# A fourth seven-product group per quarter in the MLP of a Trainium2 encoder block

## The reference

```python
h2 = rms_norm(x, norm_ffn_g[l])
u = jnp.square(jax.nn.relu(jnp.einsum('bsd,df->bsf', h2, w_up[l])))
x = x + jnp.einsum('bsf,fd->bsd', u, w_down[l])
return rms_norm(x, norm_final_g)
```

## Time and profile before

| | us |
|---|---|
| median of 3 runs (1476.1 to 1477.17) | 1476.41 |
| the profiled execution | 1476.14 |
| its span, first to last instruction | 1474.3 |
| PE busy, 6950 matmuls | 1464.3 |
| DVE busy | 1148.8 |
| ACT busy | 777.3 |

### The profile page before, as it was taken

One profiled execution on the slowest core, in us unless ns is written; L12 is line 12 of the kernel. 1 busy time (PEld: TensorE's weight loads), 2 busy tenths in 40 slices (PEclk: granted clock), 3 DMA queues, 4 the chain that ended last, 5 costly groups with the idle time before them and its releaser, 6 DMA issues.

```text
span 1474.3 us, 18847 instructions
## 1 busy us (share of the span) xinstructions
PE 1464.3 (99%) x6950; PEld 1275.4 (87%) x6950; DVE 1148.8 (78%) x1429; ACT 777.3 (53%) x998; POOL 15.0 (1%) x21
## 2 busy tenths in 40 slices
PE   9999999999999999999999999999999999999997
PEld 8888888888888888888888888888888888888886
DVE  7977887776577787777799766897787787889677
ACT  7656564444455555444445555555555555456553
POOL 0000000000000000000000000000000000000000
PEclk9999999999999999999999999999999999999999
DMA  9556544666655565565765777767867876777853
GB/s 327 195 169 208 185 154 166 229 202 239 212 183 183 190 199 175 193 203 199 245 233 182 251 248 239 234 210 240 268 204 218 265 244 226 243 221 234 283 192 127
DMA packets 163097, 317.69 MB, mean 215 GB/s; under 512 B 6752, under 2 KB 16608, under 8 KB 162784
## 3 DMA queue, kind: packets, MB, share of 16 engines
q1 hardware_dynamic: 149216, 297.51, 60.9%
q10 hardware_dynamic: 13824, 19.41, 4.6%
HBM read 306.41 MB, written 10.49 MB: 215 GB/s over the span
## 4 chain that ended last, share of the span: by engine, by line
PE 94%; DVE 3%; issue 1%; DMA 0%; ACT 0%; SPq 0%; DVEq 0%; POOLq 0%; POOL 0%; ACTq 0%
PE acc L619 83%; PE banks L856 5%; PE acc L909 3%; DVE wlo L1388 1%; PE acc L856 1%; PE banks L638 1%; PE banks L657 1%; PE banks L647 0%; DVE sum_lo L1984 0%; DMA raw<-in_w_in 0%; DVE mix L1988 0%; ACT whi L947 0%; DVE mix L1774 0%; DVE ta_lo L1994 0%; PE banks L754 0%
## 5 line engine op out<-in xcount | busy, mean ns | idle before, releaser
L947 ACT ACTIVATE whi<-raw 128x1024 fp32r<-128x1024 f32 x542 | 568.1, 1056 | 573.6 <-PE acc L619 480.9
L1388 DVE TENSOR_TENSOR wlo<-raw,whi 128x1024 fp32r<-128x1024 f32 x542 | 655.4, 1221 | 264.6 <-ACT whi L947 260.9
L619 PE MATMUL acc<-whi,ta_hi 128*128 128x512 f32 x1308 | 497.4, 380 | 0.3 <-DVE wlo L1477 0.3
L619 PE MATMUL acc<-wlo,ta_hi 128*128 128x512 f32 x1308 | 495.7, 379 | 0.0
L619 PE MATMUL acc<-whi,ta_lo 128*128 128x512 f32 x1308 | 495.7, 379 | 0.0
L619 PEld LDWEIGHTS acc<-whi,ta_hi 128*128 128x128 f32 x1308 | 247.2, 189 | 37.0 <-issue 1.8
L619 PEld LDWEIGHTS acc<-whi,ta_lo 128*128 128x128 f32 x1308 | 247.2, 189 | 35.0
L619 PEld LDWEIGHTS acc<-wlo,ta_hi 128*128 128x128 f32 x1308 | 247.3, 189 | 34.6
L619 PE MATMUL acc<-whi,tb_hi 128*128 128x512 f32 x512 | 194.2, 379 | 0.0
L619 PE MATMUL acc<-wlo,tb_hi 128*128 128x512 f32 x512 | 194.0, 379 | 0.0
L619 PE MATMUL acc<-whi,tb_lo 128*128 128x512 f32 x512 | 194.0, 379 | 0.0
(11 more groups left out here) (213 smaller groups left out, 1190.4 us busy)
## 6 DMA issues: line engine op xcount, KB each, us to landing
raw<-in_w_in SPq DMA_DIRECT2D x64, 1024.0 KB, 5.2
raw<-in_w_up SPq DMA_DIRECT2D x64, 1024.0 KB, 5.3
raw<-in_w_down SPq DMA_DIRECT2D x54, 1024.0 KB, 5.2
raw<-in_w_gate SPq DMA_DIRECT2D x32, 1024.0 KB, 5.4
raw<-in_w_att SPq DMA_DIRECT2D x16, 1024.0 KB, 5.0
raw<-in_w_ret SPq DMA_DIRECT2D x16, 1024.0 KB, 5.0
raw<-in_w_out SPq DMA_DIRECT2D x16, 1024.0 KB, 5.2
raw<-in_w_down SPq DMA_DIRECT2D x20, 512.0 KB, 4.7
```

What stands on the lines that cost most here:

```text
L619: last = nc.tensor.matmul(paired(acc[B.parity][:, t, :]), a[:, k, tok], halves_in_turn(b), start=(k == 0 and n == 0), stop=(k == (B.ends + ...
L947: nc.scalar.activation(whi[:, B.ring_at(u), :], raw[:, B.raw_at(u), :], ACT.Copy).then_inc(hi_ready, 1)
L1388: V_.tensor_tensor(wlo[:, at, :], raw[:, B.raw_at(u), :], whi[:, at, :].bitcast(f32), ALU.subtract).then_inc(lo_ready, 1)
```

## The change

`LATE` gets a third entry: up block 3 hosts columns 2 and 3 of c = 2. So J and K lose two more units each in quarters 0 to 2 (all four down blocks have 4 units), and the up block 3 of quarters 1 to 3 gets a group. Where J is short (4 units), DVE does the mixtures after J's first split, and J's second split behind them. In both fold functions the third fold goes ahead of the split of unit u+3, and in `fold_to_bank` two splits of K, not one, come ahead of folds 4 and 5. The loops over quarters 1 and 2 are written out.

```diff
-LATE = {0:(0,1,3),2:(0,1,2)}
+LATE = {0: (0, 1, 3), 2: (0, 1, 2), 3: (2, 3, 2)}
...
             stage6(0, True)
-            with pe.Fori(1, 3) as q:
+            for q in range(1, 3):
                 stage6(q, False)
             stage6(3, False, True)
...
                 split(Q.down[1], 3, 4)
+                short = Q.units[2] == 4
                 if not wide:
-                    split(Q.J, 0, 2)
+                    split(Q.J, 0, 1 if short else 2)
                 mixed_tokens(Q.turn(q, 4), q * MIXES_OF_QUARTER)
+                if short:
+                    split(Q.J, 1, 2)
                 lo_from_exchanged(q * 4 + 16, 3)
...
                 fold(1, G.k, acc[K.parity][:, 0, :], ALU.add)
-                split(E, u + 3, u + 4)
                 dve.wait_ge(product_done, G.products(2))
                 fold(0, G.k, chain, ALU.subtract)
-                part(K, 0, 1)
+                split(E, u + 3, u + 4)
+                part(K, 0, 2)
                 dve.wait_ge(product_done, G.products(3))
                 dve.wait_ge(folded, G.folds(2))
                 fold(1, G.k, chain, ALU.subtract)
                 fold(1, G.j, chain, ALU.add)
-                part(K, 1, 2)
+                part(K, 2, 3)
                 dve.wait_ge(folded, G.folds(5))
                 add_residual(E, G.j)
-                part(K, 2, K.ends + 1)
+                part(K, 3, K.ends + 1)
...
                 fold(1, G.k, third, ALU.add)
-                split(E, u + 3, u + 4)
                 dve.wait_ge(product_done, G.products(2))
                 fold(0, G.k, chain, ALU.subtract)
+                split(E, u + 3, u + 4)
                 dve.wait_ge(folded, G.folds(3))
                 fold(0, G.j, second, ALU.add)
                 split(B, 6, 7)
```

More of the change, by code:

```diff
@@ L585, in _ @@
             stage6(0, True)
-            with sp.Fori(1, 3) as q:
+            for q in range(1, 3):
                 stage6(q, False)
@@ L1360, in _ @@
             stage6(0, True)
-            with act.Fori(1, 3) as q:
+            for q in range(1, 3):
                 stage6(q, False)
@@ L1997, in _ @@
             stage6(0, True)
-            with dve.Fori(1, 3) as q:
+            for q in range(1, 3):
                 stage6(q, False)
```

## The result

The change is slower: 1484.33 us (1483.49 to 1485.24) against 1476.1 us (1476.06 to 1477.17), five runs each, a ratio of 1.0055 with a 95% interval of 1.0044 to 1.0066. The forecast was 1478.9, its range 1474.9 to 1481.7. The profiled execution took 1483.92 us, and its span is 7.8 us longer than that of before.

A forecast was written before the change was run, and what follows sets the result against it. PE was taken as the bound: matmuls times pitch, plus holes. Terms -3.9 - 1.3 + 2.5 + 1.8 + 1.7 + 1.95 - 0.1 = +2.65 us on 1476.14 gave 1478.8, stated as 1478.9, range 1474.9 to 1481.7.

The forecast's parts named there:

- The matmuls: New group on PE: 42 matmuls do what 48 did, three times, so 18 fewer, -3.9 us.
- the sixth product's holes: Six old late groups: with fold 3 ahead of the split, PE's wait before product six goes, -1.3 us.
- the tails: Units behind six late groups: split 7 is done too late for PE, 0.42 us each, +2.5 us.
- the last quarter: Quarter three keeps eight-unit down blocks; its sixth product is in time and its end gains, -0.1 us.
- The addition of DVE's line in the boundary group: Quarters one and two: DVE's instructions without a pause make PE wait 1.15 us each, against 0.3 before; +1.7 us together.
- quarter zero's boundary: Boundary group of quarter zero: the fetch lands later, so PE waits 2.4 us against 0.45 before, +1.95 us.
- the new late group: Fourth up block's group: the corner lands 5.2 us after issue, fold 2 is late, 0.6 us three times, +1.8 us.
- the paragraph on the boundary group: Boundary groups behind four J units: fetched tokens land by 1073.7, mixtures follow J's first split; +1.7 and +1.95 us.
- Transfers too late: Rival: late fetches and right corners delay DVE and PE pays one for one; 1484, with half 1481.5; chance 0.14.
- Rivals one and two: Whole kernel: half the waits, 1475.4 to 1477.4, chance 0.18; the waits don't appear, 1470 to 1473, chance 0.09.
- Rival four: Loop branches: DVE or ACT lose time at each and the change gains it, at least 3 us needed; chance 0.01.
- Loops written out: Quarters one and two: no cost or gain beyond 0.08 us per waited handoff, as PE showed no hole at the loop's start.

The follow-up runs named there:

- The two SP waits: The change with SP holding J's second load until the park has landed and the left corner's load as long as the right one's: 1477.98 us.
- the tail first: The change with the tail's two splits together, ahead of the late group's folds 5 to 7: 1485.65 us, ratio 1.006.

## Why the prediction was wrong, and where it was right

**Right.** The matmuls; the sixth product's holes, all gone in the six old late groups; the tails, 0.37 for 0.42 us each; the last quarter. The addition of DVE's line in the boundary group is right where its start is right: 1.12 us in each quarter for the 1.15 of the forecast. With the transfers in time the changed computation takes 1477.98 us, 0.9 below the forecast. That it comes so near is in part luck: there quarter zero's boundary costs 1.1 us for the forecast's 2.4, and the new late group 2.3 for 1.8. In the change as built quarter zero was too high as well (1.8 for 2.4 us), since there the mixtures start 1.2 us late, not 1.7.

**The step that failed** is in the paragraph on the boundary group: "The fetch is issued from 1067.13, its fourth part 1.3 us later, landing 5.3 at most: 1073.7". Issue and landing were taken over from before. What the changed kernel shows is 2.0 and 1.3 us later by issue, and in quarter two 2.2 us more to land. This is worth +1.1 us in quarter one and +3.8 in quarter two (1.6 of that for the lower clock). The forecast said of SP that its "loads only change places". It had DVE 0.6 us late ahead of the new group, and used that for the corner, but did not follow the lateness through: a load is released by DVE's splits, so late splits move the loads, and these are then under way beside the park. The price stood in the trace of the kernel before: of its parks from quarter one on, those with a 1 MB load 2.4 to 2.5 us ahead take 3.7 to 4.0 us, those with one 1.8 to 1.9 us ahead 4.7 to 5.0, and those with one 1.6 us ahead 5.3 to 6.8. The two SP waits put exactly this step back: the mixtures start at T0 + 15.4, and the boundaries of quarters one and two cost 1.1 us each for the forecast's 1.15. The 7.5 us of quarter two's fetch is the less certain part, since the kernel without the group has one of 7.8.

**A term too small**: the new late group, 1.8 us in the sum, 3.0 measured. The corner was issued where the sum had it, but landed after 5.7, 6.4 and 4.8 us, not 5.2; two are inside the bounds that were given (4.6 to 6.0), and each is paid almost one for one.

**The rivals.** "Transfers too late" had a chance of 0.14, with 1481.5 to 1484, and is what happened, at 0.3 us beyond its end. Its test was a fetch landing later than 1074.3 in the old clock, which is T0 + 16.0; it landed at T0 + 17.1 and T0 + 19.4. The chance was small because I asked only whether the landing would vary, as it does between quarters, and not what the change does to the loads ahead of it. Rivals one and two, with fewer waits, are refuted by the tails and the boundary holes, which are all there. Rival four, a gain from the branches, is not what the kernels without the group show: written out against a loop is 1.1 us there, not the 3 that it needed.

**"Loops written out" cost nothing** was read from a row without a hole. For the kernel without the group that is right within 1.1 us. For the change it isn't: kept as a loop it would be 8 us slower still. A branch that costs nothing before need not cost nothing after the change; the row shows only the first.

**Open.** How much of the 8 us of the loop is DVE's stall and how much PE's own, and why DVE's is longer with the group; how much of quarter two's slow fetch is chance; and why the kernel without the group is steady written out and spread as a loop.

## What to carry to other kernels

Where a transfer's issue hangs on an engine that the change makes busier, move the whole chain on paper: busier engine, ring slot, load, whatever small transfer is issued a microsecond behind that load, and the in-order queue that waits for it. If a small transfer on the critical path follows big ones, let the queue of the big ones wait until it has landed, and then look at once for who waits for the big ones. Look at what fewer matmuls cost the engine that prepares them: here 3.9 us of matmuls cost 35.5 us of VectorE work in places where VectorE had little pause left, and the best version without that trade is as fast as the best with it.

## What the runs showed of the hardware

- The fourth park of a quarter (512 KB to DRAM) takes 2.6 us when no load started less than 4.8 us ahead of it, 3.7 to 4.1 (written out without the group also 4.4 and 5.2) with a 1 MB load 2.3 to 2.5 us ahead, 4.7 to 5.7 with one 1.8 us ahead, and 5.2 to 6.2 with one 1.3 to 1.5 us ahead. A 1 MB load that goes while park and fetch are under way takes up to 9.3 us in the change and up to 10.2 in the other kernels, not 5.
- After PE had stood for 3.19 us the granted clock was 0.50 for 3.2 us, and seven matmuls cost 1.6 us more. That hole cost half as much again as its own length; around the one of 1.06 us in quarter one the granted clock was 1.00 throughout. The length of the stop alone does not tell which of the two it will be: in the run with the last folds deferred and the change's SP, a stop of 2.44 us was followed by 3.4 us at 0.50 and one of 2.34 us by none, and with the tail first 2.36 and 2.53 us, with the loop one of 2.80 us, left the clock at 1.00.
- Where a loop went back in the kernel with the loop and the new group, DVE stood for 3.9 us and PE for 2.6 and 3.0 us, with nothing in the trace that was waited for.
